# Loading the experts' gate and up weights in 2 KB pieces instead of 1 KB

## What is computed

```python
D_MODEL, N_EXPERTS, TOP_K, D_EXPERT = 1024, 32, 2, 256
...
def expert_block(args):
    xb, e = args
    return (jax.nn.silu(xb @ w_gate[e]) * (xb @ w_up[e])) @ w_down[e]
```

## Time and profile before

| | |
|---|---|
| median of 3 runs | 3389.91 us |
| lowest, highest | 3387.38, 3398.75 us |
| profiled execution, first to last instruction | 3393.5 us |
| TensorE matmuls busy | 3126.6 us, 92% |
| VectorE, ScalarE, GpSimd busy | 50%, 37%, 54% |
| moved by DMA | 491.69 MB, mean 145 GB/s |

### The profile page before, as it was taken

One profiled execution on the slowest core, in us unless ns is written; L12 is line 12 of the kernel. 1 busy time (PEld: TensorE's weight loads), 2 busy tenths in 40 slices (PEclk: granted clock), 3 DMA queues, 4 the chain that ended last, 5 costly groups with the idle time before them and its releaser, 6 DMA issues. The chain is left out here.

```text
span 3393.5 us, 56800 instructions
## 1 busy us (share of the span) xinstructions
PE 3126.6 (92%) x19621; PEld 2484.2 (73%) x19621; DVE 1687.2 (50%) x4096; ACT 1242.9 (37%) x2675; POOL 1821.2 (54%) x1447
## 2 busy tenths in 40 slices
PE   6999999899599998799799999999998996999992
PEld 4788887688598897799566666666665885899981
DVE  3555556577344333455365556555661564444333
ACT  2444445222123332444244444444442321332233
POOL 2555555244244443344488888888885222444434
PEclk8999999999799999899699999999998997999996
DMA  3001012644599996455602211221112643999986
GB/s 105 27 28 41 29 40 58 216 149 136 195 328 322 319 317 169 123 160 153 158 10 54 51 26 41 54 51 29 39 60 73 205 149 129 341 320 318 313 240 218
DMA packets 359641, 491.69 MB, mean 145 GB/s; under 512 B 87309, under 2 KB 286753, under 8 KB 357144
## 3 DMA queue, kind: packets, MB, share of 16 engines
q1 hardware_dynamic: 326136, 412.83, 38.7%
q0 software_dynamic: 33312, 76.43, 8.8%
HBM read 362.79 MB, written 135.09 MB: 147 GB/s over the span
## 5 line engine op out<-in xcount | busy, mean ns | idle before, releaser
L2185 POOL TENSOR_TENSOR keep_wg<-keep_wg,ab_pT 128x1024 f32<-128x1024 f32 (+2 forms) x320 | 597.9, 1868 | 90.7 <-ACT ab_pT L2219 48.3
L2219 ACT ACTIVATE ab_pT<-ab_S 128x512 f32<-128x512 f32 (+4 forms) x704 | 349.9, 505 | 511.8 <-PE ab_S L2317 253.7
L2246 DVE TENSOR_REDUCE ab_mx<-ab_W 128x2 f32<-128x800 f32 (+1 forms) x224 | 249.7, 1117 | 207.9 <-PE ab_W L2331 203.2
L1337 POOL DMA_INDIRECT scratch_h<-ex_y,ex_prow x65 | 104.5, 1607 | 437.2 <-ACT ex_yr L1370 258.8
L1509 PE MATMUL ex_G<-ex_xT,keep_wg 128*128 128x160 f32 x2080 | 297.3, 302 | 10.5 <-DMA ex_wu<-in_moe_w_up 10.5
L1509 PEld LDWEIGHTS ex_G<-ex_xT,keep_wg 128*128 128x128 f32 x2080 | 288.1, 192 | 12.1 <-DMA ex_wu<-in_moe_w_up 11.3
L1509 PE MATMUL ex_U<-ex_xT,ex_wu 128*128 128x160 f32 x2080 | 293.1, 299 | 0.0
L1509 PEld LDWEIGHTS ex_U<-ex_xT,ex_wu 128*128 128x128 f32 x2080 | 286.1, 190 | 0.0
L2366 PE MATMUL ab_O<-ab_pT,keep_wg 128*64 128x512 f32 (+4 forms) x1408 | 262.8, 515 | 0.0
L350 POOL TENSOR_TENSOR aa_prob<-aa_prob,aa_rden 128x1024 f32<-128x1024 f32 x68 | 127.4, 1894 | 191.6 <-DVE aa_rden L517 191.6
L1382 DVE TENSOR_TENSOR ex_wd_lo<-ex_wd,ex_wd_hi 128x2048 fp32r<-128x2048 f32 x65 | 149.0, 2292 | 160.2 <-ACT ex_wd_hi L1375 160.2
(11 more groups left out here) (325 smaller groups left out, 7954.1 us busy)
## 6 DMA issues: line engine op xcount, KB each, us to landing
keep_wg<-in_moe_w_gate SPq DMA_DIRECT2D x65, 1024.0 KB, 8.0
ex_wu<-in_moe_w_up SPq DMA_DIRECT2D x65, 1024.0 KB, 10.7
ex_wd<-in_moe_w_down SPq DMA_DIRECT2D x65, 1024.0 KB, 12.4
scratch_h<-pr_h SPq DMA_DIRECT2D x33, 512.0 KB, 5.0
scratch_xn<-pr_xn SPq DMA_DIRECT2D x33, 512.0 KB, 2.7
pr_o<-scratch_oT SPq DMA_DIRECT2D x32, 512.0 KB, 4.7
scratch_qT<-pb_qT SPq DMA_DIRECT2D x17, 768.0 KB, 5.2
scratch_oT<-keep_wg SPq DMA_DIRECT2D x17, 512.0 KB, 2.9
```

The costliest lines, as they stand in the source:

```text
L2185: nc.gpsimd.tensor_tensor(to, to, pT[:, U % RING, :, 0:n], ALU.add).then_inc(added, 1)
L2219: nc.scalar.activation(pT[:, U % RING, h, 0:n], S[:, h, 0:n], ACT.Exp, scale=B_SCALE).then_inc(exped, 1)
L2246: nc.vector.reduce_max(mx[:, :, t, c:c + 1].rearrange("p h a -> p (h a)"), W[:, j % 2, :, 0:n], AX.X).then_inc(emptied, 1)
```

## The change

The eight chunks of the input dimension are put together from other rows. Chunk c = 2a + b now holds rows 256a + 2p + b, on partition p. Two neighbouring rows of a weight matrix then stand on the same partition and beside each other in DRAM and in the tile, so a partition takes four pieces of 2 KB. The same holds for the four gate matrices loaded ahead. The tokens must be turned to match: the transpose for chunk c reads 128 columns of `x` with a step of two, starting at 256a + b; `xr` does the same within a quarter. The matmuls, their order, the tiles' sizes, all waits, and the down weights stay as they are. The number of instructions is the same.

```diff
+def piece_rows(w):
+    return w.rearrange("e (a p b) f -> e p a (b f)", p=P, b=2)
...
-                            sp.dma_start(keep["wg"][:, e, :, :],
-                                         io["moe_w_gate"][layer].rearrange("e (c p) f -> e p c f", p=P)[e]).then_inc(gate_in, 16)
+                            sp.dma_start(keep["wg"][:, e, :, :].rearrange("p (a b) f -> p a (b f)", b=2),
+                                         piece_rows(io["moe_w_gate"][layer])[e]).then_inc(gate_in, 16)
...
-                    w = io[name][layer].rearrange("e (c p) f -> e p c f", p=P)
+                    w = io[name][layer].rearrange("e (c p) f -> e p c f", p=P) if name == "moe_w_down" else piece_rows(io[name][layer])
...
-                            sp.dma_start(wg[:, e.slot4, :, :], weights_of("moe_w_gate", e)).then_inc(gu_in[e.slot4], 16)
+                            sp.dma_start(wg[:, e.slot4, :, :].rearrange("p (a b) f -> p a (b f)", b=2), weights_of("moe_w_gate", e)).then_inc(gu_in[e.slot4], 16)
...
-                        sp.dma_start(wu[:, e.slot4, :, :], weights_of("moe_w_up", e)).then_inc(gu_in[e.slot4], 16)
+                        sp.dma_start(wu[:, e.slot4, :, :].rearrange("p (a b) f -> p a (b f)", b=2), weights_of("moe_w_up", e)).then_inc(gu_in[e.slot4], 16)
...
-                                last = nc.tensor.transpose(T[:, (b + e.c) % 2, P * (c % 4):P * (c % 4) + P], x[:, e.slot4, P * c:P * c + P], ident[:, :])
+                                last = nc.tensor.transpose(T[:, (b + e.c) % 2, P * (c % 4):P * (c % 4) + P], x[:, e.slot4, :].rearrange("p (a q b) -> p a b q", a=4, b=2)[:, c // 2, c % 2, :], ident[:, :])
...
-                            last = nc.tensor.transpose(T[:, e.c % 2, P * k:P * k + P], xr[:, e.slot4, P * k:P * k + P], ident[:, :])
+                            last = nc.tensor.transpose(T[:, e.c % 2, P * k:P * k + P], xr[:, e.slot4, :].rearrange("p (q b) -> p b q", b=2)[:, k, :], ident[:, :])
```

## The result

The changed kernel takes 3400.17 us (median of 13 runs, 3394.32 to 3407.40) against 3389.91 us before it (13 runs): a ratio of 1.0025, with a 95% interval from 1.0014 to 1.0035, so 5 to 12 us more. (The quotient of the two medians alone would be 1.0030, inside that interval.) The whole interval lies above 1. The forecast was 3389 us with no change that can be told, and a range of 3377 to 3410; the time lies in that range, above the 3381 to 3396 of the forecast itself, slower by about the 0.3% at which one begins to tell.

The account below looks back on a forecast made before the run. TensorE was taken to set the pace, the DMA being full but not waited for. Steady 0, two starts -1.0, transposes 0, gates loaded ahead 0: 3389.9 - 1.0 = 3388.9, rounded 3389 us; range 3377 to 3410.

Parts of the forecast that it names:

- The steady part: Experts' gate and up loads in 2 KB pieces: 0.7 us less DMA time a period, worth 0 on the path.
- The straight line: DMA cost through 1 KB and 4 KB pieces: 11 ns a piece plus 37.5 ns a KB, 86 ns for 2 KB.
- the slack of the landings: Steady experts: gate loads land with more than 27 us to spare, so cheaper pieces gain nothing on the path.
- The two starts: Start of each layer's expert stage, where PE waits for up weights: 0.5 us a layer gained, 1.0 us for both.
- The gate matrices loaded ahead: Four gate matrices loaded while TensorE is busy: nothing waits, cost and gain 0.
- SyncE: SyncE issues the same number of DMAs and waits for TensorE at each one: cost 0.
- The transposes: Ten transposes an expert, 650 in all, reading with a step of two: taken as 0, range up to 69 us.
- rival A: Strided transposes on TensorE are slower: +17 us (3406) to +69 us (3458 with the start's gain); chance 0.13.
- B: Gathers and scatters lose their DMA share to larger pieces: 3450 us at 1 us beyond the margin; chance 0.03.
- C: The stage starts gain nearly all of their bound: -12.9 us, 3377; chance 0.06.
- D: The pieces are not larger after all, descriptors cut at 1 KB again: 3390 us; chance 0.02.

Follow-up runs that it names:

- the block: Kernel before the change plus a separate block ahead of the last stage, timing transposes and matmuls at several column steps; its whole took 3570.62 us (one run).

## Why the prediction was wrong

**The steady part (0): right.** TensorE sets the period; cheaper pieces alone gave 0.9998 and the same 13.72 to 13.74 us. The straight line gave 48 and 86 ns for packets of 1 and 2 KB, and the median packets take 46 and 84, so what a piece costs was right too. But the queue as a whole saved less: its share went from 70.6 to 67.8% with 79.35 and 78.51 MB (from 2920 to 3260 us), 3% less per byte and some 0.3 us a period, where the prediction had 0.7. The 4 KB pieces of the down loads in the same queue took longer beside the larger ones, 178 to 185 ns in the mean in place of 173. A term on which nothing waits hides such an error. The cover that the prediction named, the slack of the landings, was there.

**The two starts (-1.0 us): not found with pieces of 2 KB.** PE's wait for `ex_wu` is 10.5 us before, after, and with the pieces alone, but that they agree is luck: the second trace of the changed kernel has 12.7. Issue to first gate matmul was 0.75 shorter in one layer and 0.33 longer in the other. Over all traces it is 9.07 to 10.08 us with pieces of 1 KB and 9.14 to 10.47 with 2 KB; only with 8 KB is it shorter than all of these, 8.95 and 8.24, with the wait of 9.0 us. So a gain there is likely, from one trace of the largest pieces, but at 2 KB it is below what these runs tell.

**The gate matrices loaded ahead (0), SyncE (0): right**, as far as the pieces alone show: neither gained nor lost.

**The transposes (0): the step that failed.** The prediction asked for "the nearest row" and found L2346, a step of zero at half the clock, and took its 0. That row was wrong in both of the ways in which it was said to be far. Of the steps tried, zero is the one beside one that is free (137 ns against 140, in the block). And at 1.2 GHz (granted clock 0.50 from 886 to 889 us) strided loads cost next to nothing even here. The first eight transposes of layer 0's stage, in the trace after:

```profile
887.22 1.58 PEld L1501 LDWEIGHTS ex_T<-ex_ident,ex_x 128*128 128x128 f32 x8 [17.86 <-issue]
887.25 1.96 PE L1501 MATMUL ex_T<-ex_ident,ex_x 128*128 128x128 f32 x8 [17.79 <-DMA ex_x<-scratch_xn,ex_grow]
```

1.96 us against the 1.94 of the earlier trace rows: the gap behind the first grew from 242 to 258 ns, the others are 213 or 214 in both. At half the clock the eight cost 16 ns more, at full clock 134: such a row hides most of the cost. Measured, the term is 145 ns an expert, 14.5 ns a transpose on average, 9.4 us for 65 experts, well inside the bounds of 0 and 69 that were kept in the range; the measured ratio makes 8.5 us (4.7 to 11.9) of 3389.9. It is rival A (0.13) in a mild form. That the time still lies in the stated range is owed to that rival, for which the range was widened, and not to the forecast. The prediction set the price from which one would see it at 16 ns each; it came out just below that, and was seen.

The rule of the Trainium skill that was weighed beside it ("SBUF — State Buffer", on cachelines) gave 0 for a step of two and called four not safe. The measurements decide, and for a weight load they differ from it: 209 ns at two, 212 at four, 195 at eight, against 140. For the moving operand and for VectorE they agree with its shape: 592, 612 and 1079 ns a record at one, two and four, and VectorE's 1339, 1336 and 2327 ns at one, two and eight. The prediction carried the rule over to an operand for which no row stood behind it.

**Rivals B, C, D: not seen at 2 KB.** The pieces are larger (293081 packets in all, 66560 fewer than before), no wait on a scatter came up, and the starts didn't gain their bound. What rival B feared did come up with pieces of 8 KB, in layer 1 alone: GpSimd waited 57.7 us for its scatters, off the path. Why not in layer 0, no run shows.

**What stays open.** Why a load with a step takes some 195 to 212 ns, and why eight and three are a little cheaper than two and four, no run explains; nor why the first load of an expert starts only with its own transpose. A step of eight in the kernel cost 14 ns less an expert than worked out from the block: 9 of them are its first load, which took 185 ns where 194 had been reckoned with.

## What to carry to other kernels

Where one engine is busy without a gap, an edit that moves work to its operands is not free until a row of the same operand, the same kind of step and the same clock says so; ten instructions at 14 ns outweigh thousands of packets that nobody waited for. Put a permutation where there is slack: a step of two cost 9 us in TensorE's weight loads and nothing in one instruction of VectorE a tile, though a step of eight there cost 1 us a tile and the kernel some 12. When the effect is near the spread of the runs, read it from the period of the loop, not from two spans.

## What the runs showed of the hardware

At full clock a weight load of 128 float32 columns takes 140 ns with neighbouring columns, 137 with one column repeated, and 195 to 212 ns with steps of two, three, four and eight. Behind another transpose most of that is hidden: 109 ns from one to the next become 113 to 121 in the block. A load that starts only with its own transpose pays all of it, 57 ns at a step of two. At half the clock eight strided transposes cost 16 ns more in all. The same step on the moving operand follows another rule (429, 450, 900 and 918 ns between starts at one, two, four and eight). A DMA packet of the hardware queue took 46, 84, 159 to 164 and 309 ns in the median at 1, 2, 4 and 8 KB. The queue whose gate and up pieces grew from 1 to 2 and 8 KB took 70.6, 67.8 and 58.3% of the DMA engines for 79.35, 78.51 and 77.60 MB in the same stretch of layer 1, and TensorE's period stayed at 13.735 us.
